# Attention scores in three passes of rounded halves, and one two-tensor scaling for both heads

## What is computed

```python
q, kc, vc, ks, vs, kw, vw, gates, z = split(rmsnorm(x) @ w_in)      # q is scaled by 64 ** -0.5
s_c = q @ k_cmp.T - slope * (t - center);  p_c = masked_softmax(s_c)  # compressed keys
s_s = q @ ks.T - slope * (t - pos);        p_s = masked_softmax(s_s)  # all 8 blocks are selected
s_w = q @ kw.T - slope * (t - pos);        p_w = masked_softmax(s_w)  # window of 512
o = g0 * (p_c @ v_cmp) + g1 * (p_s @ vs) + g2 * (p_w @ vw)            # gates g = sigmoid(...)
y = (o * silu(z)) @ w_out
```

## Time and profile before

| | before |
|---|---|
| median of three runs | 1948.21 us |
| the profiled execution, its own time | 1947.58 us |
| its span, first to last instruction | 1945.8 us |
| TensorE busy | 1921.9 us (99%) |
| TensorE weight loads busy (beside the matmuls) | 1515.6 us (78%) |
| VectorE busy | 1142.8 us (59%) |
| GpSimd busy | 795.0 us (41%) |
| ScalarE busy | 578.2 us (30%) |
| mean granted TensorE clock | 0.996 |

### The profile page before, as it was taken

How to read it: one execution, slowest core, us unless ns; L and a number is a source line. 1 busy time by engine, 2 the same in 40 slices (tenths; PEclk the granted TensorE clock), 3 DMA queues, 4 the chain that set the end, 5 groups by cost and what they waited for, 6 DMA issues and landing times.

```text
span 1945.8 us, 26522 instructions
## 1 busy us (share of the span) xinstructions
PE 1921.9 (99%) x9866; PEld 1515.6 (78%) x9866; DVE 1142.8 (59%) x2077; ACT 578.2 (30%) x1118; POOL 795.0 (41%) x454
## 2 busy tenths in 40 slices
PE   8999999999999999999999999999999999999999
PEld 5967777788888776777788888886788888888887
DVE  5769998788974545676654445333654454545311
ACT  3136566316641134454221111101332221111000
POOL 3632222368854432222344444443233344444443
PEclk9999999999999999999999999999999999999999
DMA  5621101223122231111232222332112222222332
GB/s 186 185 74 34 44 34 34 77 93 102 39 72 97 92 120 55 66 66 54 66 110 94 95 95 96 108 107 89 65 65 76 76 91 96 96 97 97 107 120 76
DMA packets 54596, 167.66 MB, mean 86 GB/s; under 512 B 6864, under 2 KB 14928, under 8 KB 54112
## 3 DMA queue, kind: packets, MB, share of 16 engines
q1 hardware_dynamic: 46624, 155.21, 24.0%
q10 hardware_dynamic: 7872, 11.09, 2.0%
HBM read 157.90 MB, written 2.10 MB: 82 GB/s over the span
## 4 chain that ended last, share of the span: by engine, by line
PE 89%; DVE 8%; issue 1%; ACT 1%; DMA 0%; ACTq 0%; POOL 0%; DVEq 0%
PE bank L186 17%; PE bank L187 17%; PE bank L190 17%; PE bank L582 5%; PE bank L587 5%; PE bank L583 5%; DVE prob L1651 2%; DVE ssb L1638 2%; PE bank L1273 1%; PE bank L200 1%; PE bank L206 1%; PE bank L1298 1%; PE bank L203 1%; PE bank L2623 1%; PE bank L2612 1%
## 5 line engine op out<-in xcount | busy, mean ns | idle before, releaser
L169 POOL TENSOR_TENSOR wlo<-raw,whi 128x1024 fp32r<-128x1024 f32 x248 | 594.6, 2398 | 901.7 <-DVE whi L177 901.7
L177 DVE CAST whi<-raw 128x1024 fp32r<-128x1024 f32 x288 | 206.2, 716 | 340.3 <-PE bank L190 241.4
L186 PE MATMUL bank<-xh,whi 128*128 128x512 f32 x888 | 347.1, 391 | 0.0
L187 PE MATMUL bank<-xl,whi 128*128 128x512 f32 x888 | 345.6, 389 | 0.0
L190 PE MATMUL bank<-xh,wlo 128*128 128x512 f32 x888 | 219.4, 389 | 0.0
L186 PEld LDWEIGHTS bank<-xh,whi 128*128 128x128 f32 x888 | 166.7, 188 | 37.5 <-issue 3.1
L187 PEld LDWEIGHTS bank<-xl,whi 128*128 128x128 f32 x888 | 166.8, 188 | 34.9 <-issue 0.5
L190 PEld LDWEIGHTS bank<-xh,wlo 128*128 128x128 f32 x888 | 166.7, 188 | 34.6
L582 PE MATMUL bank<-xh,whi 128*128 128x512 f32 x424 | 175.3, 413 | 1.5 <-DVE whi L177 1.5
L583 PE MATMUL bank<-xl,whi 128*128 128x512 f32 x424 | 166.0, 392 | 0.0
L186 PE MATMUL bank<-ghi,whi 128*128 128x512 f32 x308 | 119.8, 389 | 0.0
(11 more groups left out here) (427 smaller groups left out, 3475.7 us busy)
## 6 DMA issues: line engine op xcount, KB each, us to landing
raw<-in_weights_dram SPq DMA_DIRECT2D x288, 512.0 KB, 3.2
h<-in_x_dram SPq DMA_DIRECT2D x2, 1024.0 KB, 7.1
out_dram<-h ACTq DMA_DIRECT2D x8, 256.0 KB, 2.0
etab<-in_even_tables_dram ACTq DMA_DIRECT2D x1, 1730.0 KB, 6.5
sz<-su SPq DMA_DIRECT2D x16, 64.0 KB, 2.0
sz<-su SPq DMA_DIRECT2D x16, 48.0 KB, 2.0
x_kh<-kvc_h ACTq DMA_DIRECT2D x2, 256.0 KB, 5.0
x_kl<-kvc_l ACTq DMA_DIRECT2D x2, 256.0 KB, 6.9
```

What stands on the lines that cost most here:

```text
L169: nc.gpsimd.tensor_tensor(wlo[:, s % 2, :], raw[:, s, :], whi[:, s % 2, :].bitcast(F32), ALU.subtract).then_inc(w_lo, 1)
L177: nc.vector.tensor_copy(whi[:, t_of_4 % 2, :], raw[:, t_of_4, :]).then_inc(w_hi, 1)
L186: nc.tensor.matmul(to, w_h[k], rhs_hi(k), start=first and k == 0, stop=False)
L187: nc.tensor.matmul(to, w_h[k], rhs_lo(k), start=False, stop=False)
```

## The change

The scores of the two attention branches are no longer fp32 products. Queries (`qst`) and keys (`nk`) are kept as rounded high halves, with low halves beside them (`qlow`, `nkl`), and three fp32r products replace one fp32 product: high by high, low query by high key, high query by low key, alternating between the two heads. To make the halves: for the four key tiles, VectorE writes to `sq`, ScalarE copies the rounded half to `nk`, GpSimd subtracts (`pool_keys_low`); for each pair's query, ScalarE makes a rounded and an unrounded copy, and GpSimd subtracts (`query`) ahead of the low half of the next weight tile. The scores against the compressed keys read the unrounded copy. In the scaling, the reciprocals of both heads are first multiplied by both gates in one small product, and then one tensor_tensor scales the probabilities of both heads.

```diff
-        qst = at("qst", [P, 2, S])
+        qst = at("qst", [P, 2, S], F32R)
-        nk = at("nk", [P, 4, S])
+        nk = at("nk", [P, 4, S], F32R)
@@ pe_nsa
             pe_cmp_scores(pe, 0, bank[6])
+            pe.wait_ge(n_kvh, 8)
+            pe.wait_ge(n_kl, 4 + 1)
             pe_scores(pe, 0)
@@ pe_scores
-                for hd in range(2):
-                    b = 64 * hd
-                    mm = nc.tensor.matmul(bank[2 + 2 * br + hd][:, 0:w], qst[b:b + 64, i % 2, qb * P:(qb + 1) * P],
-                                          nk[b:b + 64, 2 * br + j, 0:w], start=True, stop=True)
+                q_h, q_l = (x[:, qb * P:(qb + 1) * P] for x in (qst[:, i % 2, :], qlow[i % 2]))
+                k_h, k_l = (x[:, 0:w] for x in (nk[:, 2 * br + j, :], nkl[2 * br + j][:]))
+                for n, (q, k) in enumerate(((q_h, k_h), (q_l, k_h), (q_h, k_l))):
+                    for hd in range(2):
+                        b = 64 * hd
+                        mm = nc.tensor.matmul(bank[2 + 2 * br + hd][:, 0:w], q[b:b + 64], k[b:b + 64],
+                                              start=n == 0, stop=n == 2)
@@ pe_macro
                 if m == 3:
                     pe.wait_ge(n_c, 4 * (i + 1) + 2)
+                    pe.wait_ge(n_kl, 4 + i + 2)
@@ act_nsa
-                nc.scalar.activation(kvc[0][:, u, :], bank[4 + u % 2], ACT.Copy).then_inc(n_kvh, 1)
+                to, of = (kvc[0][:, u, :], bank[4 + u % 2]) if u < 4 else (nk[:, u - 4, :], sq[:, u % 2, :])
+                nc.scalar.activation(to, of, ACT.Copy).then_inc(n_kvh, 1)
@@
             windows(1)
+            for u in range(4, 8):
+                high(u)
@@
+            act.wait_ge(n_kl, 4)
             act_take_turned(act, "nsa_rest", 0, 4, nin, 0)
@@ act_nsa_q
-            nc.scalar.activation(qst[:, i % 2, :], acc[0][:], ACT.Copy, scale=0.125).then_inc(acc_free[r % 2], 1)
+            nc.scalar.activation(qst[:, i % 2, :], acc[0][:], ACT.Copy, scale=0.125).then_inc(n_kvh, 1)
+            nc.scalar.activation(sq[:, i % 2, :], acc[0][:], ACT.Copy, scale=0.125).then_inc(acc_free[r % 2], 1)
@@ dve_nsa
-                nc.vector.tensor_tensor(bank[4 + u % 2] if u < 4 else nk[:, u - 4, :], acc[u % 2][:], rstd[:],
+                if u >= 6:
+                    dve.wait_ge(n_kvh, u - 1)
+                    dve.wait_ge(n_kl, u - 5)
+                nc.vector.tensor_tensor(bank[4 + u % 2] if u < 4 else sq[:, u % 2, :], acc[u % 2][:], rstd[:],
                                         ALU.mult).then_inc(acc_free[u % 2], 1)
@@ dve_scale
-            for hd in range(2):
-                g = 6 * i + 3 * hd + 1 + br
-                mul = nc.vector.tensor_scalar(prob[:, br, hd, 0:w], prob[:, br, hd, 0:w], gsig[:, qb, g:g + 1],
-                                              stat[:, 8 + 2 * br + hd:9 + 2 * br + hd], ALU.mult, ALU.mult)
-            mul.then_inc(n_sc, 1)
+            nc.vector.tensor_tensor(share, share, gsig[:, qb, g:g + 4:3], ALU.mult).then_inc(n_r, 1)
+            dve.wait_ge(n_r, 4 * M + 2 * br + 2)
+            nc.vector.tensor_tensor(prob[:, br, :, 0:w], prob[:, br, :, 0:w], share.unsqueeze(2).broadcast_to([P, 2, w]),
+                                    ALU.mult).then_inc(n_sc, 1)
@@ pool_keys_low, new; for u = 4 to 7, each behind the low half of tile u + 2
+            pool.wait_ge(n_kvh, u + 1)
+            nc.gpsimd.tensor_tensor(nkl[u - 4][:], sq[:, u % 2, :], nk[:, u - 4, :].bitcast(F32), ALU.subtract).then_inc(n_kl, 1)
@@ pool_nsa; query(0) stands behind the low halves of tiles 0 to 5 and ahead of slope(0)
+            def query(i):
+                r = 3 + 2 * i if i else 4
+                pool.wait_ge(n_kvh, 8 + i + 1)
+                pool.wait_ge(acc_free[r % 2], freed(O0["nsa_rest"] + r))
+                nc.gpsimd.tensor_tensor(qlow[i % 2], sq[:, i % 2, :], qst[:, i % 2, :].bitcast(F32),
+                                        ALU.subtract).then_inc(n_kl, 1)
@@
                 if i < PAIRS - 1:
+                    query(i + 1)
                     low(7 + 2 * i)
```

More of the change, by code:

```diff
@@ L1076, in build @@
         nmix = at("nmix", [P, S])
+        after_nmix = used[0]
+        SSQ_AT = base - 4 * S
+        LNV_AT = SSQ_AT - 4 * 32 - 8 * S
+        XF_AT = LNV_AT - 8 * S
+        nkl = [at(f"nkl{u}", [P, S], F32R, offset=offset)
+               for u, offset in enumerate((XF_AT, XF_AT + 4 * S, LNV_AT, SSQ_AT))]
+        used[0] = after_nmix
+        qlow = (nh[:, KC - 1, :], nl[:, KC - 1, :])
         n_loaded = sem("n_loaded")
@@ L1083, in build @@
         n_kvl = sem("n_kvl")
+        n_kl = sem("n_kl")
         n_wgate = sem("n_wgate")
@@ L1251, in pe_cmp_scores @@
             for qb in range(QB):
-                mm = nc.tensor.matmul(to[:, qb * 2 * NW:(qb + 1) * 2 * NW], qst[:, i % 2, qb * P:(qb + 1) * P],
+                mm = nc.tensor.matmul(to[:, qb * 2 * NW:(qb + 1) * 2 * NW], sq[:, i % 2, qb * P:(qb + 1) * P],
                                       kcb[:, i // 4, :, :].rearrange("p h n -> p (h n)"), start=True, stop=True)
@@ L1646, in dve_scale @@
             dve.wait_ge(n_e, 4 * M + 2 * br + 2)
-            nc.vector.reciprocal(stat[:, 8 + 2 * br:10 + 2 * br], stat[:, 4 + 2 * br:6 + 2 * br]).then_inc(n_r, 1)
-            dve.wait_ge(n_r, 2 * M + br + 1)
-            for hd in range(2):
-                g = 6 * i + 3 * hd + 1 + br
-                mul = nc.vector.tensor_scalar(prob[:, br, hd, 0:w], prob[:, br, hd, 0:w], gsig[:, qb, g:g + 1],
-                                              stat[:, 8 + 2 * br + hd:9 + 2 * br + hd], ALU.mult, ALU.mult)
-            mul.then_inc(n_sc, 1)
+            share, g = stat[:, 8 + 2 * br:10 + 2 * br], 6 * i + 1 + br
+            nc.vector.reciprocal(share, stat[:, 4 + 2 * br:6 + 2 * br]).then_inc(n_r, 1)
+            dve.wait_ge(n_r, 4 * M + 2 * br + 1)
+            nc.vector.tensor_tensor(share, share, gsig[:, qb, g:g + 4:3], ALU.mult).then_inc(n_r, 1)
+            dve.wait_ge(n_r, 4 * M + 2 * br + 2)
+            nc.vector.tensor_tensor(prob[:, br, :, 0:w], prob[:, br, :, 0:w], share.unsqueeze(2).broadcast_to([P, 2, w]),
+                                    ALU.mult).then_inc(n_sc, 1)
         def dve_turned(dve, M, br):
@@ L1691, in dve_macro, with pool_keys_low @@
                 dve_scale(dve, M + 1, 0)
+        def pool_keys_low(pool, u):
+            pool.wait_ge(n_kvh, u + 1)
+            nc.gpsimd.tensor_tensor(nkl[u - 4][:], sq[:, u % 2, :], nk[:, u - 4, :].bitcast(F32), ALU.subtract).then_inc(n_kl, 1)
         def pool_nsa(pool):
@@ L1713, in rest @@
                 nc.gpsimd.tensor_tensor(nl[:, i, :], nmix[:], nh[:, i, :].bitcast(F32), ALU.subtract).then_inc(n_lo, 1)
+            def query(i):
[4 more added lines that the diff above has]
+                                        ALU.subtract).then_inc(n_kl, 1)
             for r in range(6):
                 low(r)
+            query(0)
             slope(0)
@@ L2853, in _ @@
                 pool_zeros(pool)
-                pool_stream(pool, 0, T0["nsa_rest"])
+                pool_stream(pool, 0, 6)
+                for u in range(4, 8):
+                    pool_low(pool, u + 2)
+                    pool_keys_low(pool, u)
+                pool_stream(pool, 10, T0["nsa_rest"])
                 pool_nsa(pool)
```

## The result

| | before | after |
|---|---|---|
| median (runs beside one another) | 1947.6 us | 1966.1 us |
| ratio after to before, 95% interval | | 1.0084 (1.0072 to 1.0096) |
| the profiled execution, its span | 1945.8 us | 1963.8 us |
| TensorE busy, its mean granted clock | 1921.9 us, 0.996 | 1932.6 us, 0.986 |
| VectorE busy | 1142.8 us | 1147.0 us |

The change makes the kernel 0.84% slower; 1951.0 was forecast, with a range from 1943 to 1958. Ten executions of the kernel after fall in two groups: eight between 1964.7 and 1970.7 us, with a mean clock of 0.986 or less, and two at 1953.0 and 1955.8 us, with 0.994 and 0.993. Something that comes or doesn't come thus costs about ten microseconds or more, and shows as the clock.

The account below looks back on a forecast made before the run. TensorE was taken to set the pace, VectorE 2.3 us a pair behind. Terms -1 + 1.8 + 1.6 + 0.4 = +2.8 us gave 1950.4 profiled, 1951.0 as median ("same"); range 1943 to 1958.

Parts of the forecast that it names:

- Ahead of the loop: keys: Before the loop, GpSimd's key subtractions block VectorE, so TensorE stalls at compression tiles: +1.8 us, bounds 0 and +3.5.
- Scores: Attention loop: a macro's scores take 0.22 us plus six rounds of two heads side by side; -0.41 us a pair.
- rival (2): Loop scores: fp32r products on half the rows don't run side by side, 12 rounds replace 6; 1977 us, chance 0.06.
- (4): Loop scores: width 256 runs at two cycles a column, +0.63 us a pair; 1956 us, chance 0.09.
- The ring: Loop pair as TensorE's and VectorE's parts between two meetings; a change in either moves it; -1 us over 7 pairs.
- -2.05 blocked before: Loop: 2.05 us a pair that GpSimd's low part blocks VectorE's 384 scalings, counted as removed from VectorE's part.
- my two meetings: Each pair: TensorE waits for VectorE before turning compressed probabilities; VectorE waits for TensorE before copying the turned 256 block.
- the won race: Loop: VectorE's large scaling product starts before GpSimd's query remainder; called a dead heat; won -0.66, lost +0.28 us a pair.
- rival (1): VectorE freed: race won in each pair, small operations before the loop let GpSimd by; 1944 us, chance 0.14.
- Loop start: GpSimd's low part of tile 6 delays VectorE's subtraction of the maxima and the turn at 133.00: +1.6 us.
- rival (3): Loop: VectorE asks 0.2 us later, its small product waits for the query remainder, +2.4 a pair; 1969 us, chance 0.08.
- rival (5): Front stalls near their upper bounds (3.5, 2.6, clock 1.5) with the race lost, +6 to +9; 1955 us, chance 0.17.

Follow-up runs that it names:

- e1: The changed kernel with two groups of small S5 set-up steps on VectorE moved behind the seventh and eighth compression tiles; 1952.03 us, 1.0019 of before.
- e7: The kernel before, nothing of the change, but GpSimd starts its low parts and mix remainder only after VectorE's scaling; 1947.87 us.
- e8: e1 with, at the loop's start, the first slopes ahead of the query remainder and tile 6's low part behind VectorE's second scaling; 1950.08 us.
- e12: e6 with the change's two-tensor scaling in place of the tensor_scalars; 1948.27 us.
- e5: e1 with the scaling undone (one tensor_scalar for each head again), scores still in three passes; 1947.12 us.
- e6: e5 with GpSimd's low parts, query remainder and mix remainder waiting for VectorE's scaling, first slopes ahead of the query remainder; 1944.17 us, 0.9981 of before.
- e3: The kernel before plus 14 redundant small products on VectorE ahead of the second compression tile's split; 1963.33 us, 1.0075 of before.
- e11: e3 with 12 redundant small products in place of 14; 1963.48 us.

## Why the prediction was wrong

The step that failed is the term "Ahead of the loop: keys". It had the right cause and nearly the right size of the stall: 0.9 forecast in front of the second compression tile, 1.56 measured, of which 0.7 come from ScalarE's DMA issues, which took 3.78 us in this execution for a group that took 3.08 before. The later, smaller stalls weren't seen, so the term of +1.8 (its parts add up to 1.9) measured +1.56; that agreement is partly luck. VectorE's next split ended at 77.87, and TensorE with tiles of 3.46 us would have asked for it at 73.67 + 3.46 = 77.13: an estimated stall of 0.7, as forecast, which the slower clock hid. But the term priced a stall as the time that it lasts. I had asked what the clock does at one place, the start of the loop, where it falls in the kernel before, and not at this one. In the place of "+1.8" stand 1.56 us of stall and 13.0 us of clock: 11.05 in the compression (12.61 less the stall) and 1.94 behind it. e1, without the stall, has them back. The trace of before could not show the effect, since no stall falls among its narrow products; but it could have bounded it: at half the clock, seven tiles of 3.45 us could take up to 24 us longer.

Without the clock's 13.0 us, +5.0 remain, against the +2.8 of the sum: 0.45 from the start of the kernel, the stall of 1.56, 1.71 at the loop's start, and 1.27 in the loop. Term by term:

- **Scores.** Three passes at the four widths take 0.82, 0.92, 1.25 and 1.59 us up to the next instruction, where 0.94, 0.94, 1.24 and 1.58 were forecast: 4.58 a pair instead of 4.70. The middle value between the bounds was right at 256 and above and a little high at 128. Heads run side by side, so rival (2) is out, and so is (4), since width 256 takes 0.92. TensorE's timeline at width 128 (each row two products, both heads) has a round every 0.11 us:

```profile
201.51 0.28 PE L1287 MATMUL bank<-nk,nh 64*128 64x128 f32 x2
201.63 0.28 PE L1287 MATMUL bank<-nkl,qst 64*128 64x128 f32 x2
201.74 0.27 PE L1287 MATMUL bank<-nk,qst 64*128 64x128 f32 x2
201.85 0.28 PE L1287 MATMUL bank<-nk,nh 64*128 64x128 f32 x2
201.96 0.27 PE L1287 MATMUL bank<-nkl,qst 64*128 64x128 f32 x2
202.17 1.09 PE L1300 MATMUL bank<-tables,prob 128*128 128x128 f32 x8
```

- **Scaling.** The large product takes 0.96 us at width 384 and 1.23 at 512. From one reciprocal to the next the scaling of 512 takes 1.53 us (200.15 to 201.68) instead of 1.11, 0.42 more; 0.45 was forecast.
- **The ring.** -1 was forecast for the loop, +1.3 measured (+0.02, +0.51, +0.74), inside the bounds of -5 and +2, but the reasoning had a flaw. "-2.05 blocked before" credited VectorE's part with the lock, and that part doesn't run unbroken from one of my two meetings to the other: there are two more turns of TensorE in it, at which VectorE waits once it is freed (1.63 and 0.23 us in e7). What is freed ahead of such a turn is idle time there and not a gain. For the same reason the 28.75 us that e7 expected as TensorE's own work weren't reached. Against the kernel before, the won race gained nothing, so rival (1), 1944 us, had a wrong mechanism, though the race of its condition was won in each pair; its other condition, small operations that let GpSimd by, failed.
- **The end of the loop.** The +0.74 us are a loss with the same cause as in the pairs: in the last pair nothing but attention is left beside the turns, and TensorE waits 1.76 us where it waited 0.71, and 0.65 where it waited 0.24. The forecast had no term for it. In the profiled executions of e1, e8 and e12 (not in those of the kernel after, e5 and e6) the clock falls there for 3.4 us: in e1 at 361.0, and this stretch takes 33.12 us; in e8 and e12 at 354.5 and 353.6, and it takes 31.5, as in the kernel after. Why it falls there, and what sets the moment, stays open.
- **Loop start.** +1.6 was forecast, +1.71 measured, and e8 shows the cause. (The working lets the subtraction end near 132.1; against its end before, 130.87, that would be only 1.2.) Of the +0.4 for the clock nothing came: it is at 0.50 for 6.83 us in both kernels.
- **Rivals.** By the number rival (3), 1969 us, came nearest to 1966.1, and that is chance: its small product that waits for the query remainder didn't come, as the race was won. By the place it was rival (5), the front stalls near their upper bounds, 1955 us, but by their length; no case had the clock fall in the compression. Nor did either sign come by which the forecast would have been wrong: VectorE was blocked by the key subtractions, and the scores follow the six rounds. What was missing is a rival in which a stall among narrow products brings the clock down, priced by the bound above.

## What to carry to other kernels

Work that is moved on a side engine has to be followed to the point where it makes TensorE wait, and there the question is not only how long, but among which products: a microsecond of waiting in a long stretch of narrow ones cost over ten here (e3, e11). Slack that one link of a ring gains is lost at the next place where the two engines meet, so list all meetings of a loop before a freed engine is credited with anything. And of a bundle of two edits each should be built alone: here the three passes with the old scaling, GpSimd's work held back and the small S5 steps moved are 0.2% faster than before (e6), while the bundle as it was built is 0.8% slower.

## What the runs showed of the hardware

- The clock stays at 0.50 through 33 us of uninterrupted 160-column products (75.34 to 108.53), with TensorE busy all the time, and comes back 4.4 us after the products of 512 columns have begun. The same products, begun at 1.00 and not interrupted, run through at 1.00.
- At the lower clock the narrow products follow one another every 0.20 to 0.21 us instead of 0.14 to 0.15, so they lose about a third of their rate at half the clock: a compression tile takes 5.1 instead of 3.45 us.
- A product of 2 columns, 0.16 us alone, takes 2.36 us when GpSimd starts first (L1673 at 179.88 in the kernel after). The Trainium skill, page "SBUF — State Buffer", section "Who interferes with whom", says that the order of issue, not the shape of the operation, decides who is blocked; the trace agrees, down to 0.04 us: at 193.65 VectorE starts first, its product takes 0.96 us and GpSimd's next operation 2.06 instead of 1.39.
- Products on half of the rows in pairs take 0.11, 0.12, 0.17 and 0.23 us a round at widths 128, 256, 384 and 512: near one column a cycle of 2.4 GHz from 256 up (0.107, 0.16 and 0.213 us), and above it at 128 (0.053).
